# Eight rounds of a chunked recurrence: mask operations for two blocks at once, and the scans moved into the levels

## What is computed

```python
def step(state, inp):
    r_t, w_t, k_t, v_t, kk_t, a_t = inp
    sa = jnp.einsum('bhvk,bhk->bhv', state, -kk_t)
    state = (state * w_t[:, :, None, :]
             + sa[..., None] * (kk_t * a_t)[:, :, None, :]
             + v_t[..., None] * k_t[:, :, None, :])
    y = jnp.einsum('bhvk,bhk->bhv', state, r_t)
    return state, y
_, y = lax.scan(step, state0, xs)
```

## Time and profile before

| | |
|---|---|
| median of 3 runs | 3028.71 us (3028.18 to 3035.36) |
| profiled execution: its own time / its span | 3027.78 us / 3026.1 us |
| granted clock of TensorE over the span | 0.97 |
| TensorE matmul busy | 2840.3 us (94%) |
| VectorE busy | 1979.2 us (65%) |
| POOL busy | 1511.4 us (50%) |
| ScalarE busy | 1378.5 us (46%) |

### The profile page before, as it was taken

The page is one execution under the profiler, slowest core; times in us unless marked ns, Lnnn a source line. Parts: engine busy times, 40 slices in busy tenths (PEclk is TensorE's granted clock), DMA queues, the critical chain, the costliest instruction groups (busy, mean ns, idle before and its releaser), DMA issues.

```text
span 3026.1 us, 61868 instructions
## 1 busy us (share of the span) xinstructions
PE 2840.3 (94%) x25236; PEld 2248.9 (74%) x25236; DVE 1979.2 (65%) x2811; ACT 1378.5 (46%) x2298; POOL 1511.4 (50%) x1009
## 2 busy tenths in 40 slices
PE   8899999978999999999999999999888899999998
PEld 6544566856877878876688788888876688888887
DVE  6587895888787877786034255665546856665667
ACT  5475977134334333436333355455423434433445
POOL 0001000445776667764367346554364667767772
PEclk9799999989999999999999999999988999999999
DMA  9100000712222233221533212211131111112111
GB/s 316 43 1 15 2 2 2 250 42 75 84 92 83 69 94 100 83 85 56 195 117 120 99 46 67 82 60 53 36 100 30 56 42 56 57 41 66 45 56 70
DMA packets 194440, 225.98 MB, mean 75 GB/s; under 512 B 14863, under 2 KB 151650, under 8 KB 194210
## 3 DMA queue, kind: packets, MB, share of 16 engines
q1 hardware_dynamic: 182529, 180.66, 18.9%
q10 hardware_dynamic: 11680, 42.01, 3.8%
HBM read 185.15 MB, written 37.22 MB: 73 GB/s over the span
## 4 chain that ended last, share of the span: by engine, by line
PE 59%; DVE 10%; issue 10%; POOL 8%; ACT 3%; DMA 1%; SPq 0%; POOLq 0%; DVEq 0%; ACTq 0%
PE ps L148 13%; PE ps L149 13%; PE ps L150 13%; POOL w_lo L710 4%; PE ps L3707 3%; PE ps L3719 2%; PE ps L2226 1%; PE ps L2215 1%; PE ps L2237 1%; PE ps L3632 1%; POOL w_room L704 1%; DVE uc L1033 1%; PE ps L3756 1%; PE ps L3746 1%; DVE x_lo L998 1%
## 5 line engine op out<-in xcount | busy, mean ns | idle before, releaser
L148 PE MATMUL ps<-x_hi,w_hi 128*128 128x512 f32 x1232 | 494.7, 402 | 54.8 <-DVE x_lo L998 21.6
L149 PE MATMUL ps<-x_lo,w_hi 128*128 128x512 f32 x1232 | 486.7, 395 | 0.0
L150 PE MATMUL ps<-x_hi,w_lo 128*128 128x512 f32 x1232 | 486.6, 395 | 0.0
L710 POOL TENSOR_TENSOR w_lo<-w_room,w_hi 128x512 fp32r<-128x512 f32 x200 | 312.2, 1572 | 246.7 <-ACT w_hi L1178 246.4
L710 POOL TENSOR_TENSOR w_lo<-sq_room,w_hi 128x512 fp32r<-128x512 f32 x188 | 291.0, 1558 | 176.6 <-ACT w_hi L1178 176.4
L1033 DVE SCALAR_TENSOR_TENSOR uc<-u,pc,uc 128x1024 f32<-128x1024 f32 x176 | 329.1, 1880 | 24.1 <-ACT uc L1182 13.7
L148 PEld LDWEIGHTS ps<-x_hi,w_hi 128*128 128x128 f32 x1232 | 235.3, 191 | 127.4 <-issue 23.9
L1021 DVE TENSOR_TENSOR u<-u,ps 128x512 f32<-128x512 f32 x264 | 174.4, 683 | 188.8 <-PE ps L150 164.4
L150 PEld LDWEIGHTS ps<-x_hi,w_lo 128*128 128x128 f32 x1232 | 235.6, 191 | 50.5
L149 PEld LDWEIGHTS ps<-x_lo,w_hi 128*128 128x128 f32 x1232 | 236.1, 192 | 46.5
L148 PE MATMUL ps<-g_hi,w_hi 128*128 128x512 f32 x640 | 249.7, 390 | 0.6 <-DVE h L1099 0.5
(11 more groups left out here) (448 smaller groups left out, 6800.7 us busy)
## 6 DMA issues: line engine op xcount, KB each, us to landing
w_room<-in_f_w_up_dram SPq DMA_DIRECT2D x48, 512.0 KB, 5.0
rwkv_scratch<-rp_stage ACTq DMA_DIRECT2D x48, 512.0 KB, 3.5
sq_room<-in_f_w_up_dram SPq DMA_DIRECT2D x40, 512.0 KB, 4.9
ada_w<-in_ada_w_dram SPq DMA_DIRECT2D x80, 256.0 KB, 2.9
rc_raw<-rwkv_scratch SPq DMA_DIRECT2D x32, 512.0 KB, 3.8
d_ada_w<-in_ada_w_dram SPq DMA_DIRECT2D x24, 512.0 KB, 7.6
d_r<-in_ada_w_dram ACTq DMA_DIRECT2D x24, 512.0 KB, 5.7
sq_room<-in_f_w_down_dram SPq DMA_DIRECT2D x24, 512.0 KB, 4.3
```

Source lines behind the costliest of these rows:

```text
L148: pe.matmul(out, w_hi, x_hi, start=first, stop=False, skip_group_check=skip)
L149: pe.matmul(out, w_hi, x_lo, start=False, stop=False, skip_group_check=skip)
L150: return pe.matmul(out, w_lo, x_hi, start=False, stop=last, skip_group_check=skip)
L710: pool.tensor_tensor(slot_of(k.w_lo, s), src, slot_of(k.w_hi, s).bitcast(F32), ALU.subtract).then_inc(w_lo_done, 1)
```

## The change

- Removed and key products of two blocks (twins) lie side by side in their bank pairs, and are issued one behind the other. One mask operation serves both: `removed_dve`, a new `inverse_dve` (the masked copy, until now the second half of `removed_dve`) and `key_dve` are each called for even x only, on 512 elements a partition instead of 256. The mask table `first` holds its first two masks twice for that.
- TensorE's order in a pair of blocks is now: chain 2x, transposes x, chain 2x+1, keys x and x+1, chain 2x+2, removed x+2 and x+3, chain 2x+3, transposes x+1. Both first removed products stand ahead of the loop. VectorE's is: masks, state 2x, inverse, state 2x+1, key masks, states 2x+2 and 2x+3.
- Log decays and running sums have two rooms each, for even and odd rounds (`w_ins`, `cums`). The scans for round p+2 are called in level 2 of round p, behind each of the two mask operations. Round 1's are called in round 0's front at x = 0 and 2. `load_w(p + 2)` stands ahead of `load_v(p + 1)` on SP; the odd room overlaps memory of the projections, so `load_w(1)` waits for their last matmul. The small sums `sm` move to another place.
- In round 0 ScalarE's wait for the projections' stores stands behind the copies of block 4 instead of ahead of those of block 0.

The diff, cut (left out are the places where `w_in` and `cum` become `w_ins[q % 2]` and `cums[q % 2]`, the columns that the products are written to, and the counts of semaphores):

```diff
-    sb("room", [P, 2, S])
+    odd = sb("odd", [P, 2, S])
...
+    cum_even = sb("cum", [P, S])
+    w_ins, cums = (w_even, odd[:, 0, :]), (cum_even[:, :], odd[:, 1, :])
...
     def load_w(sp, q):
-        sp.wait_ge(sem["ar0"], q)
-        sp.dma_start(w_in, scr[W_, q, :, :]).then_inc(sem["w_ld"], 16)
+        if q >= 2:
+            sp.wait_ge(sem["ar0"], q - 1)
+            sp.wait_ge(sem["scan"], 2 * q)
+        sp.dma_start(w_ins[q % 2], scr[W_, q, :, :]).then_inc(sem["w_ld"], 16)
...
         load_k(sp, 1)
-        load_w(sp, 1)
         load_a(sp, 1)
         load_r(sp, 1)
+        sp.wait_ge(*pair0.values_done)
+        load_w(sp, 1)
         pair0.all_stored(sp)
         for p in range(PAIRS):
             if p + 1 < PAIRS:
                 if p:
                     load_r(sp, p + 1)
+            if p + 2 < PAIRS:
+                load_w(sp, p + 2)
+            if p + 1 < PAIRS:
                 load_v(p + 1)
             if p + 2 < PAIRS:
                 load_k(sp, p + 2)
-                load_w(sp, p + 2)
                 load_a(sp, p + 2)
...
     def scan_dve(dve, q, i):
         dve.wait_ge(sem["w_ld"], 16 * q + 16)
-        dve.wait_ge(sem["bt"], q)
-        dve.wait_ge(sem["kt"], q)
-        dve.tensor_tensor_scan(cum[:, halves(i)], carry[:, halves(i)], w_in[:, halves(i)], 0.0, ALU.mult, ALU.add
+        if q >= 2:
+            dve.wait_ge(sem["bt"], q - 1)
+            dve.wait_ge(sem["kt"], q - 1)
+        dve.tensor_tensor_scan(cums[q % 2][:, halves(i)], carry[:, halves(i)], w_ins[q % 2][:, halves(i)], 0.0,
+                               ALU.mult, ALU.add
...
     def removed_pe(pe, p, x):
-        u, g = p % 2, planes(REMOVED, 4)
-        if x:
-            pe.wait_ge(sem["g2_sb"], 2 * (BLK * p + x))
-        else:
+        u, g, twin = p % 2, planes(REMOVED, 8), x % 2
+        if x == 0:
             pe.wait_ge(sem["ar1"], p + 1)
             pe.wait_ge(sem["ar0"], p + 1)
             pe.wait_ge(sem["bt"], p + 1)
             if p:
                 pe.wait_ge(sem["q_sb"], 4 * p)
+        elif twin == 0:
+            pe.wait_ge(sem["g2_sb"], BLK * p + x)
+        before_at, after_at = (slice((4 + 2 * i + twin) * C64, (5 + 2 * i + twin) * C64) for i in range(2))
...
     def key_pe(pe, p, x):
-        u, g = p % 2, planes(KEYS, 2)
-        if x:
-            pe.wait_ge(sem["g3_sb"], BLK * p + x)
-        else:
+        u, g, twin = p % 2, planes(KEYS, 4), x % 2
+        if x == 0:
             pe.wait_ge(sem["kt"], p + 1)
             if p:
                 pe.wait_ge(sem["sx"], 2 * p)
+        elif twin == 0:
+            pe.wait_ge(sem["g3_sb"], (BLK * p + x) // 2)
...
+    def twins(i):
+        return two(i)[:, :, 0:2 * P].rearrange("p h (x c) -> p x h c", x=2)
+
     def removed_dve(dve, p, x):
-        dve.wait_ge(sem["g2_ps"], BLK * p + x + 1)
-        g = planes(REMOVED, 4)
-        both = upper[:, 0:2, :].rearrange("p i c -> p (i c)").unsqueeze(1).to_broadcast([P, 2, P])
-        dve.tensor_tensor(tg[:, x, :, G_M:G_BR + 1, :].rearrange("p h i c -> p h (i c)"), g[:, :, 0:P], both,
+        dve.wait_ge(sem["g2_ps"], BLK * p + x + 2)
+        both = upper[:, 0:2, :].rearrange("p i c -> p (i c)").unsqueeze(1).unsqueeze(1).to_broadcast([P, 2, 2, P])
+        dve.tensor_tensor(tg[:, x:x + 2, :, G_M:G_BR + 1, :].rearrange("p x h i c -> p x h (i c)"), twins(REMOVED), both,
                           ALU.mult).then_inc(sem["g2_sb"], 1)
+
+    def inverse_dve(dve, p, x):
+        dve.wait_ge(sem["g2_ps"], BLK * p + x + 2)
         if x == 0:
             dve.wait_ge(sem["id_sb"], 3 * p + 2)
-        src = g[:, :, :].rearrange("p h (i c) -> p i h c", c=C64)[:, 2:4, :, :]
-        dve.copy_predicated(ul[:, :, :, x, :], first[:, 0:2, :].unsqueeze(2).to_broadcast([P, 2, 2, C64]), src
+        src = planes(REMOVED, 8)[:, :, 2 * P:4 * P].rearrange("p h (i c) -> p i h c", c=P)
+        chosen = first[:, 0:4, :].rearrange("p (i x) c -> p i (x c)", x=2).unsqueeze(2).to_broadcast([P, 2, 2, P])
+        dve.copy_predicated(ul[:, :, :, x:x + 2, :].rearrange("p i h x c -> p i h (x c)"), chosen, src
                             ).then_inc(sem["g2_sb"], 1)
 
     def key_dve(dve, p, x):
-        dve.wait_ge(sem["g3_ps"], BLK * p + x + 1)
-        both = upper[:, 2:4, :].rearrange("p i c -> p (i c)").unsqueeze(1).to_broadcast([P, 2, P])
-        dve.tensor_tensor(tg[:, x, :, G_KA:G_KR + 1, :].rearrange("p h i c -> p h (i c)"), planes(KEYS, 2), both, ALU.mult
-                          ).then_inc(sem["g3_sb"], 1)
+        dve.wait_ge(sem["g3_ps"], BLK * p + x + 2)
+        both = upper[:, 2:4, :].rearrange("p i c -> p (i c)").unsqueeze(1).unsqueeze(1).to_broadcast([P, 2, 2, P])
+        dve.tensor_tensor(tg[:, x:x + 2, :, G_KA:G_KR + 1, :].rearrange("p x h i c -> p x h (i c)"), twins(KEYS), both,
+                          ALU.mult).then_inc(sem["g3_sb"], 1)
...
         for p in range(PAIRS):
             if p:
                 transposes_pe(pe, p, 0)
-                removed_pe(pe, p, 0)
-            else:
-                removed_pe(pe, p, 0)
+            for twin in range(2):
+                removed_pe(pe, p, twin)
+            if p == 0:
                 pe.wait_ge(pair0.read, pair0.reads[1])
                 transposes_pe(pe, p, 0)
-            for x in range(BLK):
+            for x in range(0, BLK, 2):
                 if p:
                     chain_pe(pe, p - 1, 2 * x)
-                key_pe(pe, p, x)
-                if x + 1 < BLK:
-                    removed_pe(pe, p, x + 1)
+                if x:
+                    transposes_pe(pe, p, x)
                 if p:
                     chain_pe(pe, p - 1, 2 * x + 1)
-                if x + 1 < BLK:
-                    transposes_pe(pe, p, x + 1)
+                for twin in range(2):
+                    key_pe(pe, p, x + twin)
+                if p:
+                    chain_pe(pe, p - 1, 2 * x + 2)
+                if x + 2 < BLK:
+                    for twin in range(2):
+                        removed_pe(pe, p, x + 2 + twin)
+                if p:
+                    chain_pe(pe, p - 1, 2 * x + 3)
+                transposes_pe(pe, p, x + 1)
             if p + 1 < PAIRS:
                 sums_pe(pe, p + 1)
...
         eye_act(act, slice(2, 3))
-        pair0.all_stored(act)
         for p in range(PAIRS):
             q = p + 1
             more = q < PAIRS
             for x in range(BLK):
                 copies_act(act, p, x)
+                if p == 0 and x == BLK // 2:
+                    pair0.all_stored(act)
...
-            for x in range(BLK):
+            for x in range(0, BLK, 2):
                 removed_dve(dve, p, x)
                 if p:
                     state_dve(dve, p - 1, 2 * x)
+                inverse_dve(dve, p, x)
+                if p:
+                    state_dve(dve, p - 1, 2 * x + 1)
                 key_dve(dve, p, x)
                 if more and x == 4:
                     rkw_dve(dve, q)
-                if p == 0 and x in (1, 2):
-                    scan_dve(dve, 1, x - 1)
+                if p == 0 and x in (0, 2):
+                    scan_dve(dve, 1, x // 2)
                 if p:
-                    state_dve(dve, p - 1, 2 * x + 1)
+                    state_dve(dve, p - 1, 2 * x + 2)
+                    state_dve(dve, p - 1, 2 * x + 3)
             if p:
                 for i in range(2):
                     s1_dve(dve, p - 1, i)
...
+                    if p + 2 < PAIRS and lv == 2:
+                        scan_dve(dve, p + 2, s)
...
             given_dve(dve, p)
-            if p + 2 < PAIRS:
-                for i in range(2):
-                    scan_dve(dve, p + 2, i)
```

46 lines of the change are left out of this document (24 added, 22 removed).

## The result

The changed kernel takes **3052.49 us** (median of 8 runs, 3040.5 to 3056.09) against 3028.44 of the kernel before (8 runs, 3018.19 to 3035.36) measured beside it: a ratio of 1.0074 with a 95% interval of 1.0059 to 1.0089. That is slower by 0.74%, 24 us. The forecast was 3036 with a range to 3043.

The account below looks back on a forecast made before the run. Fronts were taken as bound by TensorE, with VectorE near, and in the new order by bank 6's 1.41 us. Terms 1.2 + 3.1 + 3.5 - 2.0 + 1.5 = +7.3 on 3027.8, the median 0.9 higher: 3036, range to 3043.

Parts of the forecast that it names:

- The order of TensorE (18.5 a front): From the end of `rc_sx` to the first `rc_same` matmul: neighbouring transposes wait 1.41 us for bank 6, so 18.5 us.
- the walk: Step-by-step timing of three engine queues through one front at full clock: new order 18.5 us, old 16.9 with scans, 14.9 without.
- Fronts of rounds 3 and 5 (+3.1), and 1, 2, 4 and 6 (+1.2): 18.5 us each against 16.9 and 17.0, and against 18.1 to 18.3 with half clock assumed gone: +3.1 and +1.2 in sum.
- Loads ("`load_w` stands ahead of `load_v` ... Nothing"): SP's queue: issuing the log decays' load ahead of the values' load costs nothing, its semaphores being long up.
- half clock in each front: Rival: many short TensorE waits put every front, rounds 1 to 7, at half clock for a stretch; +9.1 us, 3045; chance 0.2.
- Scans (13.5 us off the fronts): Twelve scans leave VectorE in the fronts of rounds 1 to 6: 2.25 us a round, 13.5 if nothing else held the front.
- Scans in the levels (+1.5): Level 2, six rounds: the first scan delays the second mask operation to 2.42 us, costing 0.25 us each, +1.5.
- the prediction's last rival: Levels' own half-clock stretches may fall elsewhere: 3 us either way, taken as within the range; no chance given.
- Round 0 (-2.0): ScalarE's first copies no longer wait for the stores, so the sums come earlier: -3.5 at full clock, -1.0 at half, -2.0 taken.
- Round 7 (+3.5): Last round's front: `rc_y_n`'s copy follows the copies of transposes 7 and begins at 18.4 us against 14.9, +3.5.

Follow-up runs that it names:

- after_quiet: Changed kernel with early loads of r and w, and the store of y and g's load one front later in SyncE's order; 3043.93 us, 1.0056 of the kernel before.
- loads_early: Changed kernel with r loaded two rounds and w three rounds ahead, issued in the levels instead of at the front's start; 3044.82 us, 1.0071 of the kernel before.
- spread_early: Changed kernel with r and w loaded early in the levels and both blocks' transposes spread apart on TensorE; 3026.06 us, 1.0005 of the kernel before.
- rooms_early: Changed kernel without its order by twos (fronts block by block), with r and w loaded early in the levels; 3016.39 us, 0.997 of the kernel before.
- rooms_quiet: rooms_early with the store of y and g's load one front later in SyncE's order; 3018.3 us, 0.9975 of the kernel before.
- twins_only: Changed kernel with the scans back in the front ahead of the first masks, order by twos and both rooms kept; 3051.04 us, 1.0078 of the kernel before.
- w_late: Changed kernel with load_w(p + 2) put behind load_v(p + 1) on SP; 3044.5 us, 1.0049 of the kernel before.
- loads_early_again: loads_early unchanged, run on one chip with a repeat of the changed kernel; 3046.26 us, 1.0059 of the kernel before.
- pad32: Changed kernel with 32 small unused matmuls added in TensorE's idle time of round 0, shifting its later instructions; 3056.37 us, 1.01 of the kernel before.
- rooms: Changed kernel without its order by twos: two rooms, scans in levels, loads and round 0 as changed, products and masks block by block; 3022.47 us, 0.9985 of kernel before.
- after_third: Changed kernel repeated unaltered as the measure on the fourth group's chip; 3053.75 us, 1.0083 of the kernel before.

## Why the prediction was wrong

- **The order of TensorE (18.5 a front): right.** The 1.41 us between neighbouring transposes, the copies that release them and the last transposes at 17 us are in the trace, and after_quiet has fronts of 18.0 to 19.4. The sums wait 0.8 us for bank 6 in each of rounds 1 to 6. The experiments show the size three ways: loads_early over spread_early by 18.8 us (19 forecast for that run); the order by twos over block by block by 28.4 us with the early loads (loads_early against rooms_early; the walk has 7 x 3.7 = 26), and by 25.6 with no burst at the front's start (after_quiet against rooms_quiet).
- **Fronts of rounds 3 and 5 (+3.1), and 1, 2, 4 and 6 (+1.2): wrong, and this is the step that failed.** "I walked all three queues through a front at full clock" took for granted that TensorE always has its instructions. The forecast put this wait at nothing without naming it; the changed kernel's fronts have 12.8 us of it, and half clock where none was forecast. Rounds 3 and 5 have two waits of about 2 us each for their instructions and some 2.6 us lost in 6.8 us of half clock, 25.3 and 25.0 for 18.5: 13.3 of the 17.1 us by which the fronts exceed the forecast. The walk over the old front hit its 16.9 because the scans' pause of 2.36 us lay over the same waits; it could not tell a front with hidden waits from one without any (twins_only brings the pause back, and 3.7 us of them are left to see). The rows that showed them before, 1.5 us of `issue` in round 3's front and 1.2 in round 5's, I had not weighed.
- **Loads ("`load_w` stands ahead of `load_v` ... Nothing"): wrong.** As a matter of who waits for the data it costs nothing. As traffic it does. Before, w's load went out in the tail (at 1888.04 ahead of round 3's front, landed at 1891.60), and only g and r at the front's start (1899.62 and 1899.98). Now g, r and w go out within 0.9 us of each other there (1896.19, 1896.56 and 1897.09). w_late gives back about 7 us; loads_early gave nothing clear by its first ratio and 7.5 us beside the changed kernel on one chip; and the unread copies cost 13 to 14.
- **The rival "half clock in each front" (3045, 0.2)** came nearest in size, but by another mechanism. Half clock came in rounds 3 and 5 (in the repeats of the changed kernel in rounds 2 and 3, and in 1, 3, 4 and 5), and not from the short waits for bank 6: loads_early has all of those, and its two profiles have none in the fronts. In the changed kernel it came behind waits of 1.0 to 2.2 us for instructions, but not behind each: loads_early_again's round 3 has one of 2.1 us and pad32's round 1 one of 2.2, and both fronts stay at full clock. What decides between them is open. In all, the changed kernel's fronts have as much half clock as before (13.7 us); the forecast had assumed it gone.
- **Scans (13.5 us off the fronts): off, as said, but for one more reason.** Even block by block the move gives only 5 us, round 0's change included, because waits for instructions fill the place. With early loads the two together are worth 7 and 14 us on two chips (rooms_early against the kernel before).
- **Scans in the levels (+1.5): too small.** The mask ends when forecast (2.40 for 2.42 us); levels and tails rose by 4.4, of which 2.4 are TensorE's waits behind that mask. Half clock in levels and tails went from 13.7 to 20.5 us, which at 1.3 us for each 3.4 is an estimate of 2.6; the prediction's last rival had allowed 3 us for it. That would close the rest, but it is not shown: rooms has 4.6 us of waits behind that mask and the same 20.5 us of half clock, and its levels still sum to less than before (334.6), because their `issue` waits are shorter (17.8 us against 25.0).
- **Round 0 (-2.0): at its better end.** 3.8 us less from `rc_z` to the sums, clock 1.00; the rest of the 7.1 us is an earlier start of `rc_z` (by 3.3 us). That start lies between 1714.2 and 1729.1 us in the 18 traces, and at 1718.2 and 1729.1 in two executions of one kernel (loads_early), so this is not put down to the change.
- **Round 7 (+3.5): right**, 18.1 for 18.4. The merged masks run 0.68 to 0.69 us and the masked copy 0.73, as the earlier trace rows said.

Sum by its own terms: +7.3 forecast, of which round 0 gave 1.8 more; waits for instructions and half clock added 17.1, levels 2.9; the earlier start (-3.3) and the stretch behind the recurrence (+1.7) close it to 23.9.

## What to carry to other kernels

An engine that stands still behind another may be hiding waits of its own. Before a pause is priced as pure gain, look in the same stretch for its `issue` waits and ask which of them would lie bare. And price a transfer twice: for who waits for its data, and for what else must pass the DMA engines meanwhile, the program included; on a stretch where TensorE is the bound, try the bulk loads elsewhere, and count what comes back there: moving them out of the fronts took 13 us off the fronts in the profiles and 7.5 off the time (loads_early_again against after_third).

Where one bank has a fixed turn-round (here 1.41 us from one block's transposes to the next), spread its users over the queue before anything is merged by twos.
